# Router logits as column-group partial sums, and a first round whose table is read without the counts, in one step of a two-layer streaming encoder

## Chip, cores and metric

The kernel runs on one core of a Trainium2 chip, in one launch that takes the whole inference step. The metric is device time in microseconds (us) of that core; lower is better. All data are float32, so each matmul of the program stands in the trace as two records.

## What is computed

One step of an encoder with DEPTH = 2 layers, for 512 prompt tokens and 32 sample tokens (544 rows of 1024). A layer is a combined input projection, three parallel mixers (differential attention, retention, convolution), an output projection with a layer norm, a mixture of experts, a second layer norm and a gated side input. The part that the change touches is the router and what follows from it:

```python
def moe(x, w_router, b_router, w_exp_gate, w_exp_up, w_exp_down):
    logits = (x @ w_router) + b_router            # (544, 16), w_router (1024, 16)
    scores = softmax(logits).reshape(N, 4, 4)
    # best group of four experts by the sum of its two best scores,
    # then the two best experts inside it, weights w = their scores / their sum
    for e in range(16):
        h = silu(x @ w_exp_gate[e]) * (x @ w_exp_up[e])
        y = y + gates[:, e:e + 1] * (h @ w_exp_down[e])
```

## The kernel before, in words

The rows are held as five tiles of the token axis: four of 128 rows and one of 32 (tile 4, the sample). Everything is ordered by hand: each engine runs its own list, and semaphores join them. The engines are PE (TensorE), ACT (ScalarE), DVE (VectorE), POOL (GpSimd) and SP (SyncE, which issues nearly all weight loads, 1 MB each).

**From the output projection to the router.** For each tile, in the order 0, 1, 4, 2, 3 (`MIX_ORDER`), PE computes the output projection in two halves (`product(t, n)`, L1131), DVE adds the residual and normalises the row tile (L1894, L1611 to L1621), PE transposes it (`turn_tile`, L852) and ACT copies the transpose into `xT` (`x1_turned`, L1363). Then `logits(t)` (L1116) multiplies: eight matmuls with the tile's transposed activations as the stationary operand (128 columns, 32 for tile 4) and the 16 columns of the router's weights `w_rt` as the moving one. Between them PE does `turn_prow` (L1172) and `project(t)` (L1181), products for the gated side input. PE's list has `product(2,0)`, `logits(0)`, `product(2,1)`, `logits(1)`, `product(3,0)`, `logits(4)`, `product(3,1)`, then the transposes of tile 2, `turn_prow`, `logits(2)`, `project(0)`, the transposes of tile 3, `logits(3)`, `project(1)`, `project(2)`.

**From the logits to the table.** DVE picks the experts (from L1936), PE counts and ranks the picked rows (`rank`, L1212 to L1214, behind `project(2)` on PE's list), DVE makes seat numbers and a table `ctl` (from L1957), and signals `routed` (L2032). A round of the expert stage treats two half tiles of 64 rows, a front one (slots of `ring`) and a back one (`back` in `region`); experts are walked from 0 upwards at the front and from 15 downwards at the back. `ctl` holds the number of rounds done so far (word 0), the number of rounds of this layer less one (word 1), and per round the front expert, the back expert and two flags that say whether each is new. `mid` is word 1, `base` word 0. There are 25 rounds in the two layers together.

**SP around the first round.** Before `routed`, SP has loaded experts 0 and 15 (`early`, L649 and L651), but for the back half of the down weights. After `routed` it loads `base` and `mid` into registers (L678, L679), waits for the four gate transfers (`hold` on `b_full`, `z_full`), and then `part_of("gate", 0)` reads four table words (L681) and issues four conditional loads (L693, L694), each behind a `hold` on the signal that the buffer has been read; a load whose flag is zero moves nothing but still signals. The same follows for "up". Then come the back down loads (L651), the wait for all down transfers, three loads of norm parameters (L708 to L710) and the loop over the other rounds. PE's first `gate(0)` (L1262, L1263) waits for the signals of the conditional gate loads, and each later product for those of its own round.

```python
hold(routed, l + 1)
base = e.value_load(ctl[0:1, 0:1], min_val=0, max_val=MAXROUND * (DEPTH - 1))
mid = e.value_load(ctl[0:1, 1:2], min_val=MINROUND - 1, max_val=MAXROUND - 1)
```

## Time and profile before

| What | Value |
| --- | --- |
| median of 3 runs | 1571.17 us (1570.41 to 1574.28) |
| profiled execution, its own time | 1564.81 us |
| its span | 1563.0 us |
| granted TensorE clock, mean over the span | 0.97 |
| PE matmul busy | 1431.6 us (92%), 6900 records |
| DVE busy | 574.2 us (37%) |
| ACT busy | 271.2 us (17%) |
| POOL busy | 118.0 us (8%) |
| DMA | 326.24 MB, mean 209 GB/s |

The span is the time between the first and the last instruction of the profiled execution; some 1.8 us lie around it. "Busy" counts the engine's own instructions, whether or not anything waits for them. The three timed runs are some 6 us longer than the execution that was profiled. Layer 0's stage from output projection to table ends at about 396.6 us of the span, layer 1's at about 1167.7 us; the expert stages follow them.

### The profile page before, as it was taken

What the parts mean: (1) busy time and instruction counts of PE and PEld (TensorE: products, weight loads), DVE (VectorE), ACT (ScalarE), POOL (GpSimd) and SP (SyncE); (2) the same over time, 40 slices, a digit from 0 to 9 for tenths busy, and PEclk for the clock granted to TensorE, in tenths of its full rate; (3) what the DMA queues carried; (4) which work ended last, traced back from release to release, by engine and by line L of the source; (5) the groups of instructions that cost most, each with busy time, mean ns of one, the idle gap of its engine ahead of it and who ended that gap; (6) DMA issues with size and microseconds to landing.
All of it is one profiled execution on the core that took longest, in us unless ns stands there. A gap on an engine that the chain in (4) does not pass through costs nothing.

```text
span 1563.0 us, 20264 instructions
## 1 busy us (share of the span) xinstructions
PE 1431.6 (92%) x6900; PEld 753.4 (48%) x6900; DVE 574.2 (37%) x1144; ACT 271.2 (17%) x655; POOL 118.0 (8%) x133
## 2 busy tenths in 40 slices
PE   7999998999899999995999999979979999978688
PEld 3786356554344444332458854555543444323244
DVE  5085874254210111005522958553441111001156
ACT  1201243212100100010121023431121100000112
POOL 2100001010100000004000000010100000000120
PEclk9999998999999999997999999999999999999889
DMA  8623011343399989997033221023434899999731
GB/s 292 225 97 124 1 54 58 135 178 136 136 377 424 386 312 391 427 424 259 1 123 106 85 84 54 3 75 145 179 121 164 335 340 365 426 427 426 286 123 44
DMA packets 81802, 326.24 MB, mean 209 GB/s; under 512 B 12652, under 2 KB 15012, under 8 KB 56396
## 3 DMA queue, kind: packets, MB, share of 16 engines
q1 hardware_dynamic: 67492, 278.47, 46.2%
q0 software_dynamic: 9136, 29.16, 5.1%
q10 hardware_dynamic: 5112, 17.80, 2.8%
q8 instruction: 37, 0.61, 0.2%
q14 instruction: 25, 0.20, 0.0%
HBM read 429.19 MB, written 30.19 MB: 294 GB/s over the span
## 4 chain that ended last, share of the span: by engine, by line
PE 76%; DMA 9%; issue 5%; DVE 4%; SPq 3%; ACT 2%; DVEq 1%; POOL 0%; ACTq 0%
PE psum L1262 15%; PE psum L908 11%; PE psum L1289 8%; PE psum L967 7%; PE psum L1323 7%; PE psum L1131 7%; DMA region<-in_w_exp_up_dram 5%; PE psum L882 4%; DMA region<-in_w_exp_gate_dram 2%; PE psum L852 2%; DMA region<-in_w_exp_down_dram 2%; PE psum L1181 2%; PE psum L831 1%; PE psum L1263 1%; SPq L681 1%
## 5 line engine op out<-in xcount | busy, mean ns | idle before, releaser
L1262 PE MATMUL psum<-ring,xT 128*64 128x512 f32 x800 | 359.2, 601 | 21.8 <-DMA region<-in_w_exp_gate_dram 9.0
L1263 PE MATMUL psum<-region,xT 128*64 128x512 f32 x800 | 360.3, 602 | 0.0
L1262 PEld LDWEIGHTS psum<-ring,xT 128*64 128x64 f32 x800 | 107.8, 139 | 228.0 <-issue 228.0
L1289 PE MATMUL psum<-ring,region 128*64 128x512 f32 x400 | 179.8, 602 | 10.3 <-DMA region<-in_w_exp_down_dram 5.7
L1290 PE MATMUL psum<-region 128*64 128x512 f32 x400 | 180.0, 602 | 0.0
L908 PE MATMUL psum<-xT,ring 128*128 128x272 f32 x768 | 176.5, 393 | 0.0
L908 PEld LDWEIGHTS psum<-xT,ring 128*128 128x128 f32 x768 | 145.8, 190 | 30.1
L2058 DVE COPY region<-psum 128x512 f32<-128x512 f32 x25 | 17.3, 692 | 341.2 <-PE psum L1290 341.2
L967 PE MATMUL psum<-ring,xT 128*128 128x512 f32 (+1 forms) x288 | 132.5, 603 | 7.2 <-DVE region L1733 7.2
L1323 PE MATMUL psum<-ring,xT 128*128 128x512 f32 x256 | 115.8, 610 | 1.5 <-issue 1.5
L746 POOL TENSOR_TENSOR rr<-rq,half 128x1 f32<-128x1 f32 (+3 forms) x39 | 54.8, 1406 | 754.6 <-DVE rq L1601 278.6
L1289 PEld LDWEIGHTS psum<-ring,region 128*64 128x64 f32 x400 | 54.9, 139 | 116.4 <-issue 116.1
L1263 PEld LDWEIGHTS psum<-region,xT 128*64 128x64 f32 x800 | 107.7, 138 | 0.0
L1683 DVE SCALAR_TENSOR_TENSOR region<-region,hwT 128x574 f32<-128x574 f32 x120 | 92.6, 814 | 4.5
L2048 DVE TENSOR_TENSOR region<-region,psum 128x512 f32<-128x512 f32 x25 | 17.2, 688 | 192.0 <-PE psum L1263 192.0
L967 PEld LDWEIGHTS psum<-ring,xT 128*128 128x128 f32 (+1 forms) x288 | 49.2, 181 | 75.4 <-issue 62.7
L1323 PEld LDWEIGHTS psum<-ring,xT 128*128 128x128 f32 x256 | 49.4, 196 | 61.1 <-issue 58.8
L1363 ACT ACTIVATE xT<-psum 128x512 f32<-128x512 f32 (+1 forms) x60 | 29.5, 531 | 239.8 <-PE psum L852 239.3
L852 PE MATMUL psum<-ident,x 128*128 128x128 f32 (+1 forms) x240 | 31.9, 279 | 35.4 <-issue 34.7
L1363 ACT ACTIVATE region<-psum 128x512 f32<-128x512 f32 (+5 forms) x74 | 35.2, 519 | 156.5 <-PE psum L919 60.3
L1131 PE MATMUL psum<-ring,region 128*128 128x512 f32 x128 | 60.3, 615 | 1.4 <-ACT region L1492 0.7
L882 PE MATMUL psum<-ring,xT 128*128 128x512 f32 x128 | 59.9, 621 | 0.7 <-issue 0.7
(260 smaller groups left out, 1489.0 us busy)
## 6 DMA issues: line engine op xcount, KB each, us to landing
region<-in_w_exp_gate_dram SPq DMA_DIRECT2D x54, 1024.0 KB
ring<-in_w_exp_gate_dram SPq DMA_DIRECT2D x54, 1024.0 KB
region<-in_w_exp_up_dram SPq DMA_DIRECT2D x54, 1024.0 KB
ring<-in_w_exp_up_dram SPq DMA_DIRECT2D x54, 1024.0 KB
ring<-in_w_exp_down_dram SPq DMA_DIRECT2D x54, 1024.0 KB
region<-in_w_exp_down_dram SPq DMA_DIRECT2D x54, 1024.0 KB
ring<-in_w_in_dram SPq DMA_DIRECT2D x24, 1024.0 KB, 7.4
expert_results<-region ACTq DMA_DIRECT2D x25, 512.0 KB
```

The lines of the kernel that those rows point to most:

```text
L852: m = pe.transpose(B(key)[:, q * ROWS[t]:(q + 1) * ROWS[t]], x[0:ROWS[t], t, (4 * s + q) * P:(4 * s + q + 1) * P], ident[0:ROWS[t], 0:ROWS ...
L882: m = pe.matmul(B(key)[0:ROWS[t], :], xT[:, kc, span(t)], slot(u)[:, kc % 4, :], start=kc == 0, stop=kc == KC - 1)
L908: m = pe.matmul(B(key)[:, 0:HALF], w, xT[:, kc, half * HALF:(half + 1) * HALF], start=kc == 0, stop=kc == KC - 1)
L967: m = pe.matmul(bank[g - 1][0:ROWS[t], :], xT[:, 4 * half + kc, span(t)], slot(w)[:, kc, :], start=half == 0 and kc == 0, stop=half == 1 a ...
L1131: m = pe.matmul(B(key)[0:ROWS[t], :], mixT[kc][:, span(t)], slot(u)[:, kc % 4, :], start=kc == 0, stop=kc == KC - 1)
L1262: pe.matmul(bank[b][front, :], xeT[:, kc, front], ring[:, BLOCK_SLOT[u], kc % 4, :], start=kc == 0, stop=kc == KC - 1)
L1263: m = pe.matmul(bank[b][last, :], xeT[:, kc, last], back[:, UNIT_ROOM[u], kc % 4, :], start=kc == 0, stop=kc == KC - 1)
L1289: pe.matmul(bank[5 + half][front, :], hT[:, 2 * n + q, front], ring[:, BLOCK_SLOT[u], 2 * q + half, :], start=n + q == 0, stop=n + q == 2)
L1290: m = pe.matmul(bank[5 + half][last, :], hT[:, 2 * n + q, last], back[:, UNIT_ROOM[u], 2 * q + half, :], start=n + q == 0, stop=n + q == 2)
L1323: m = pe.matmul(B(key)[0:ROWS[t], :], xT[:, kc, span(t)], slot(u)[:, kc % 4, :], start=kc == 0, stop=kc == KC - 1)
L1363: sc.activation(dst, src, func).then_inc(free[use(key)], 1)
L1683: m = ve.scalar_tensor_tensor(cT[:, s, :], src, hwT[:, s, 32 + j:33 + j], cT[:, s, :], ALU.mult, ALU.add)
```

## The change

Router: `w_rt` is padded with zeros to 32 columns per chunk and becomes the stationary operand; `xT` becomes the moving one (128 columns, 32 for tile 4). The eight chunks go to four column groups of the array, two chunks accumulated in each, so that four partial sums stand in 4 x 32 partitions of one PSUM bank (`part_sums`). ACT copies them into SBUF (`parts_copied`), and one more matmul with the copy as stationary operand and a constant of four stacked identities, `gather4`, as moving one adds the four parts and turns them (`logits`). The new copy of tile t is issued on ACT behind `x1_turned(t)`, and PE has other work between `part_sums(t)` and `logits(t)`, except for tile 3.

SP: `base` is no longer read but carried in a register from the layer before (`rounds_done`); the holds on the gate transfers stand ahead of the wait for `routed`; the holds on read buffers are left out for round 0; `mid` is read just ahead of the loop. Around it: one more memset on POOL and one more small constant load on SP at the start, SP's wait for the memsets moved ahead of the constants' loads, and two small buffers and two counting semaphores put together.

```diff
+    c["gather4"] = (np.arange(P)[:, None] % 32 == np.arange(NE)[None, :]).astype(np.float32)
...
-        w_rt = sb("w_rt", [P, KC, NE])
+        w_rt = sb("w_rt", [P, KC, 32])
+        gather4 = sb("gather4", [P, NE])
...
+                base = rounds_done
+                for n in range(2):
+                    hold(b_full[BLOCK_SLOT[("gate", n)]], 16 * (base + l + 1))
+                    hold(z_full[BLOCK_SLOT[("gate", n)]], 16 * (base + l + 1))
                 hold(routed, l + 1)
-                base = e.value_load(ctl[0:1, 0:1], min_val=0, max_val=MAXROUND * (DEPTH - 1))
-                mid = e.value_load(ctl[0:1, 1:2], min_val=MINROUND - 1, max_val=MAXROUND - 1)
...
-                        hold(read, base + k + 1)
+                        if not first:
+                            hold(read, base + k + 1)
...
                 e.dma_start(bple, a["b_ple_gate"][L].to_broadcast([P, D])).then_inc(ln2p_in, 16)
+                mid = e.value_load(ctl[0:1, 1:2], min_val=MINROUND - 1, max_val=MAXROUND - 1)
+                rounds_done = base + mid + 1
...
+            pl.memset(w_rt[:], 0.0)
...
-                def logits(t):
+                def part_sums(t):
                     for s in range(2):
                         turned(l, ("x1", t, s))
-                    key = ("logit",)
-                    if t == MIX_ORDER[0]:
+                    key, r, n = ("logit",), ROWS[t], MIX_AT[t]
+                    if n == 0:
                         room(l, key)
+                    else:
+                        pe.wait_ge(lp_done, TILES * l + n)
                     pe.sem_inc(pe_pass, 1)
-                    for kc in range(KC):
-                        m = pe.matmul(B(key)[0:ROWS[t], NE * t:NE * t + NE], xT[:, kc, span(t)], w_rt[:, kc, :], start=kc == 0, stop=kc == KC - 1)
-                    if t == MIX_ORDER[-1]:
+                    for j in range(2):
+                        for g in range(4):
+                            m = pe.matmul(B(key)[32 * g:32 * g + 32, P:P + r], w_rt[:, 2 * g + j, :], xT[:, 2 * g + j, span(t)], start=j == 0, stop=j == 1)
+                    m.then_inc(lp_full, 1)
+
+                def logits(t):
+                    key, r, n = ("logit",), ROWS[t], MIX_AT[t]
+                    pe.wait_ge(lp_done, TILES * l + n + 1)
+                    pe.sem_inc(pe_pass, 1)
+                    m = pe.matmul(B(key)[0:r, NE * t:NE * t + NE], part_logits[:, n % 2, 0:r], gather4[:], start=True, stop=True)
+                    if n == TILES - 1:
                         m.then_inc(full[use(key)], 1)
...
+                def parts_copied(t):
+                    n = MIX_AT[t]
+                    sc.wait_ge(lp_full, TILES * l + n + 1)
+                    sc.activation(part_logits[:, n % 2, 0:ROWS[t]], bank[LOGIT_BANK][:, P:P + ROWS[t]], ACT.Copy).then_inc(lp_done, 1)
```

PE's list from `product(2,1)` of layer 0 on, before:

```order
L1116 MATMUL psum<-w_rt,xT 128x16 x8
L852 MATMUL psum<-ident,x 128x32 x8
L1131 MATMUL psum<-ring,region 128x512 x4
L1131 MATMUL psum<-ring,xT 128x512 x4
L1116 MATMUL psum<-w_rt,xT 32x16 x8
L1131 MATMUL psum<-ring,region 128x512 x4
L1131 MATMUL psum<-ring,xT 128x512 x4
L852 MATMUL psum<-ident,x 128x128 x8
L1172 MATMUL psum<-ident,region 128x128 x8
L1172 MATMUL psum<-ident,region 128x32 x2
L1116 MATMUL psum<-w_rt,xT 128x16 x8
L1181 MATMUL psum<-region 128x512 x4
```

The same stretch in the change, where L864, L1153, L1194 and L1203 are the lines that were L852, L1131, L1172 and L1181:

```order
L1138 MATMUL psum<-gather,region 128x16
L1131 MATMUL psum<-xT,w_rt 32x128 x8
L864 MATMUL psum<-ident,x 128x32 x8
L1153 MATMUL psum<-ring,region 128x512 x4
L1153 MATMUL psum<-ring,xT 128x512 x4
L1138 MATMUL psum<-gather,region 128x16
L1131 MATMUL psum<-xT,w_rt 32x32 x8
L1153 MATMUL psum<-ring,region 128x512 x4
L1153 MATMUL psum<-ring,xT 128x512 x4
L1138 MATMUL psum<-gather,region 32x16
L864 MATMUL psum<-ident,x 128x128 x8
L1194 MATMUL psum<-ident,region 128x128 x8
```

Each group of eight router matmuls keeps its place; the adding matmul of a tile stands one product later, that of tile 2 behind `project(0)`, and that of tile 3 directly behind its part sums.

SP's list from the last early load to the first conditional one, before:

```order
L649 DMA ring<-in_w_exp_down_dram 128x2048 x2
L678 TENSOR_LOAD ctl
L678 ISA x2
L679 TENSOR_LOAD ctl
L679 ISA x2
L508 ISA
L681 TENSOR_LOAD ctl
L681 ISA x2
```

and in the change, there and ahead of the loop:

```order
L654 DMA ring<-in_w_exp_down_dram 128x2048 x2
L688 TENSOR_LOAD ctl
L688 ISA x2
...
L719 DMA region<-in_b_ple_gate_dram 128x1024
L720 TENSOR_LOAD ctl
L720 ISA x2
L722 UNCONDITIONAL_BRANCH
```

One load of `ctl` and its register work are gone, and the other stands behind the parameter loads.

## Rows read from the trace of the kernel before

**Rows 1.** The page, part 4: shares of the chain that ended last.
```profile
PE 76%; DMA 9%; issue 5%; DVE 4%; SPq 3%; ACT 2%; DVEq 1%; POOL 0%; ACTq 0%
```

**Rows 2.** Timeline of PE, layer 0: start, length, engine, line, operation, count, idle before.
```profile
328.99 1.06 PE L831 MATMUL psum<-ring,region 128*32 128x128 f32 x32
329.87 1.06 PE L831 MATMUL psum<-ring,xT 128*32 128x128 f32 x32
330.85 1.09 PE L852 MATMUL psum<-ident,x 128*128 128x128 f32 x8
...
338.65 1.85 PE L1116 MATMUL psum<-w_rt,xT 128*128 128x16 f32 x16
340.35 1.07 PE L852 MATMUL psum<-ident,x 128*128 128x128 f32 x8
...
357.58 0.68 PE L1116 MATMUL psum<-w_rt,xT 128*32 128x16 f32 x16
358.19 3.70 PE L1131 MATMUL psum<-ring,region 128*128 128x512 f32 x8
...
367.24 1.96 PE L1116 MATMUL psum<-w_rt,xT 128*128 128x16 f32 x16
369.05 3.68 PE L1181 MATMUL psum<-region 128*128 128x512 f32 x8
372.56 1.04 PE L852 MATMUL psum<-ident,x 128*128 128x128 f32 x8
374.44 1.93 PE L1116 MATMUL psum<-w_rt,xT 128*128 128x16 f32 x16 [0.84 <-ACT xT L1363]
```

**Rows 3.** Timeline of DVE, layer 0, tile 3's norm, first router operation, first after the rank.
```profile
369.58 1.28 DVE L1621 SCALAR_TENSOR_TENSOR x<-x,rr,region 128x1024 f32<-128x1024 f32 x1 [0.44 <-POOL rr L746]
...
376.40 0.22 DVE L1936 TENSOR_TENSOR region<-psum,b_rt 128x64 f32<-128x64 f32 x1 [5.52 <-PE psum L1116]
...
385.24 0.17 DVE L1957 TENSOR_SCALAR ints<-psum 128x16 int32<-128x16 f32 x1 [3.50 <-PE psum L1214]
```

**Rows 4.** Timeline of ACT, layer 0: second copy of tile 3's transpose, first half of gathered rows.
```profile
373.73 0.60 ACT L1363 ACTIVATE xT<-psum 128x512 f32<-128x512 f32 x1
...
399.21 0.60 ACT L1537 ACTIVATE xT<-psum 128x512 f32<-128x512 f32 x1 [2.79 <-PE psum L1241]
```

**Rows 5.** Groups by line and form: an ACT pass of 128 columns out of PSUM.
```profile
L1340 ACT ACTIVATE region<-psum 128x128 f32<-128x128 f32 x32 | 8.4, 286 | 0.0
```

**Rows 6.** Chain that ended last, layer 0 behind the table: start, length, what.
```profile
396.64 0.47 SPq L678
...
397.46 0.28 SPq L679
...
398.03 0.05 SPq L508
...
398.41 0.26 SPq L681
...
406.85 7.39 DMA region<-in_w_exp_down_dram
...
434.11 12.62 DMA region<-in_w_exp_gate_dram
```

**Rows 7.** Timeline of PE, starts of expert products that waited for SP's loads.
```profile
401.49 1.09 PE L1262 MATMUL psum<-ring,xT 128*64 128x512 f32 x1 [1.88 <-DMA region<-in_w_exp_gate_dram]
...
446.97 0.61 PE L1262 MATMUL psum<-ring,xT 128*64 128x512 f32 x1 [0.88 <-DMA region<-in_w_exp_gate_dram]
...
1191.87 0.61 PE L1262 MATMUL psum<-ring,xT 128*64 128x512 f32 x1 [0.37 <-DMA region<-in_w_exp_gate_dram]
```

**Rows 8.** PE by stretches: length, busy, granted clock, DMA share, GB/s.
```profile
376.00:380.00 4.00, 4.00 (x9) 0.59 0.01 4
1120.00:1124.00 4.00, 4.00 (x6) 0.60 0.14 33
600.00:700.00 100.00, 93.86 (x440) 0.99 1.01 424
```

More of the change, by code:

```diff
@@ L703, in _ @@
                     for n in range(2):
-                        hold(b_full[BLOCK_SLOT[(name, n)]], 16 * (base + l + 1))
-                        hold(z_full[BLOCK_SLOT[(name, n)]], 16 * (base + l + 1))
+                        if name != "gate":
+                            hold(b_full[BLOCK_SLOT[(name, n)]], 16 * (base + l + 1))
+                            hold(z_full[BLOCK_SLOT[(name, n)]], 16 * (base + l + 1))
                     if name != "down":
-                        part_of(name, 0)
+                        part_of(name, 0, True)
                 e.dma_start(lnp_near[:, 0, :], a["ln2_g"][L].to_broadcast([P, D])).then_inc(ln2p_in, 16)
@@ L750, in _ @@
             pl.memset(ones[:], 1.0)
-            pl.memset(hw[:], 0.0).then_inc(hw_zero, 1)
-            pl.memset(zero, 0.0).then_inc(zeroed, 1)
+            pl.memset(w_rt[:], 0.0)
+            pl.memset(hw, 0.0).then_inc(hw_zero, 1)
+            pl.memset(zero, 0.0).then_inc(hw_zero, 1)
             pl.iota(iota[:], [[1, P]], base=0, channel_multiplier=0, allow_small_or_imprecise_dtypes=True)
@@ L1187, in _ @@
                 product(2, 0)
-                logits(0)
+                part_sums(0)
                 turn_tile(l, "x1", x1_ready, 1)
                 product(2, 1)
-                logits(1)
+                logits(0)
+                part_sums(1)
                 turn_tile(l, "x1", x1_ready, 4)
                 product(3, 0)
+                logits(1)
+                part_sums(4)
+                product(3, 1)
                 logits(4)
-                product(3, 1)
                 turn_tile(l, "x1", x1_ready, 2)
@@ L1199, in _ @@
                     turn_prow(t)
+                part_sums(2)
+                project(0)
                 logits(2)
-                project(0)
                 turn_tile(l, "x1", x1_ready, 3)
+                part_sums(3)
                 logits(3)
@@ L1515, in _ @@
                     sample_out("wo", n)
-                for t in MIX_ORDER[:-1]:
+                def parts_copied(t):
+                    n = MIX_AT[t]
+                    sc.wait_ge(lp_full, TILES * l + n + 1)
+                    sc.activation(part_logits[:, n % 2, 0:ROWS[t]], bank[LOGIT_BANK][:, P:P + ROWS[t]], ACT.Copy).then_inc(lp_done, 1)
+                for n, t in enumerate(MIX_ORDER[:-1]):
                     x1_turned(t)
+                    if n < 3:
+                        parts_copied(t)
                 for t in range(TILES):
@@ L1712, in _ @@
                 filled(l, key)
-                ve.tensor_copy(tails[:].rearrange("p a b -> p (a b)"), B(key)[0:CW - 1, :]).then_inc(free[use(key)], 1)
+                ve.tensor_copy(tails.rearrange("p a b -> p (a b)"), B(key)[0:CW - 1, :]).then_inc(free[use(key)], 1)
                 ve.drain()
```

25 lines of the change are left out of this document (15 added, 10 removed).

## The prediction

> **What bounds the kernel now.** I read the shares of the chain that ended last first, then the timelines around the router, then SP's part of the chain. The chain is three quarters PE; SP's own instructions hold 3% of it and DMA 9% [rows 1]. So PE's time counts wherever PE has no gap, and SP's where PE waits for a load signal.
>
> In the stage ahead of the table PE runs without a gap from product to product; the first idle time is 0.84 us ahead of the last router group, where it waits for ACT's copy of tile 3 [rows 2]. DVE has tile 3's norm done at 369.58 + 1.28 = 370.86, but PE transposes that tile only at 372.56 [rows 2, 3]: PE is 1.7 us late, so what PE saves ahead of that point arrives in full. Behind the logits PE is late again: DVE waited 3.50 us for the rank, which stands behind two projections on PE's list [rows 3]. From there DVE alone leads to the table, and then SP to PE: `gate(0)` starts at 401.49, 1.88 us after PE had nothing to do, because SP's signals come at that time [rows 7].
>
> **Router, per tile.** A 128-row group takes its slot from 338.65 to 340.35, 1.70 us for 16 records, 0.106 us each [rows 2]. For tile 1, which is followed by transposes of 32 rows, I add 0.10 for the change of shape (below): 1.80. Tile 4's group holds 357.58 to 358.19, 0.61, plus 0.10 on each side: 0.81. Tile 2's holds 367.24 to 369.05, 1.81 [rows 2].
>
> The new groups are not in the trace, but their like is: the sample's projections use 32 stationary columns in four column groups with 128 moving ones. 32 such records go from 328.99 to 329.87, 0.88 us, and the last 32 up to the next shape take 330.85 - 329.87 = 0.98 [rows 2]. So 16 records are 0.44, and a change of shape costs 0.10. One comes at each end: 0.64 per part sum. The same matmuls in sequence at the old group's 0.106 per record would take 1.70, the other bound of a group. Tile 4's part sums (32 moving columns) I take at 0.44 too, since 16 records of 16 columns behind 32 stationary ones held 0.61 with their edges. The adding matmul has the old group's shape: two records, 0.21; that of tile 4 with 32 stationary columns, two records and two edges, 0.27.
>
> *Here a rule speaks against the change.* The Trainium skill, "TensorEngine Tiling (Array Packing)", section Tiling Modes, says that a change of tiling mode drains TensorE. The trace agrees in kind, and its price is the 0.10 us above. The same page, under Performance Considerations, has a matmul of one column take as long as one of 60. An estimate from it, at 2.4 GHz, is 16 x 60 / 2400 = 0.4 us for the old group too, and the change would then gain nothing on PE. The slot of 1.70 us says otherwise, so the row decides.
>
> *Up to the end of `product(3,1)`*: before 1.70 + 1.80 + 0.81 = 4.31. After: 0.64, then 0.21 + 0.64, then 0.21 + 0.64 = 2.34. Saved 1.97. *Then up to tile 3's transposes*: before 1.81; after 0.27 + 0.64 + 0.21 = 1.12. Saved 0.69; PE is 1.7 - 0.7 = 1.0 us late there and so still decides. *Tile 3*: before, from the end of ACT's copy (373.73 + 0.60 = 374.33) to DVE's first operation (376.40) 2.07 us [rows 3, 4]. After: start of PE 0.11 later (as 374.44 stands to 374.33), 0.44 with the length of the last record 0.18 (1.06 - 0.88), signal 0.07, ACT's copy 0.286 [rows 5], start 0.11, two records 1.93 - 14 x 0.106 = 0.45, signal 0.03: 1.68. Saved 0.4. ACT has nothing queued ahead of that copy but tile 3's own, and its four other new copies lie under a product or projection of PE. The 3.50 us that DVE waits for the rank is cover: PE's projections behind tile 3 start earlier by the same 0.4. **Sum 3.1 us a layer**; the end bounds are 1.5 (the shape changes three times as dear) and 4 (no edges at all).
>
> **SP, per layer.** From 396.64 to 398.41 lie two table loads and four holds, 1.77 us [rows 6]. The first load behind the wait costs 0.47 where a later one costs 0.26; that surcharge of 0.21 goes to whichever load is first, so 1.56 are saved. The holds are (398.41 - 398.08) / 4, some 0.08 each, and four more go from the first gate and up parts: 0.3. Back comes `mid`, 398.03 - 397.46 = 0.57, behind the parameter loads. So `gate(0)`'s signals come 1.56 + 0.08 = 1.64 earlier, at 399.85; the first half of the gathered rows is turned and copied at 399.21 + 0.60 = 399.81 [rows 4], and that ties: nothing beyond 1.6 could be had. The down loads are issued 1.86 earlier and last 7.39 as before [rows 6]; SP waits for them, then does its parameter loads, `mid` and the loop. From there SP is 1.86 - 0.57 = 1.3 ahead.
>
> That smaller number decides. In layer 1 SP's signal sets `gate(1)` at 1191.87, with 0.37 us of idle PE before it; in layer 0 SP's run of instructions goes on to the gate load of round 2, issued at 434.11, which lands 12.62 later and lets PE start at 446.97 after 0.88 us of idling [rows 6, 7]. PE's own 1.6 is more than 1.3 in both. **1.3 us a layer**, between 0 (the start of the stage is hidden by something I don't see) and 1.6.
>
> **Whether it lasts.** Later in a layer the loads fill the DMA engines, 1.01 of them over 600 to 700 us, at 424 GB/s [rows 8]. Each of these loads is released by PE's reading of the buffer before it, and the stretch starts from PE's own pace, so I let the whole chain shift. If a fixed rate from a fixed start held, SP's start of that stream moves by the same 1.3.
>
> **Costed at nothing.** The extra memset and the constant's small load at the start: PE first reads either at 338.65 [rows 2], and SP's weight loads behind them, pushed back by one issue, are covered by the input projections before; if that cover is gone, an issue or two, under 2 us once, is the price. The shared buffers and semaphores change no order.
>
> **Sum.** 2 x (3.1 + 1.3) = 8.8 us. The profiled execution took 1564.81, so 1556.0 by that; the three runs have their median 6.4 us above it, so **1562.4** against 1571.17.
>
> **Rivals.**
> - *The clock gives back more.* PE has a granted clock of 0.59 over 376 to 380 and 0.60 over 1120 to 1124, that is 1.2 GHz for most of it, each time behind a router group [rows 2, 8]. With (1 - 0.59) x 4 = 1.6 us lost in each, 1.6 to 3.3 more is saved if the shorter groups end one or both: 1559 to 1561. For it: they stand behind just the work that shrinks. Against: the idle time ahead of tile 3's group stays, and a new one of some 0.5 us joins it behind the part sums, which could as well bring such a stretch.
> - *Only half arrives.* If another wait sits behind PE in the router stage (DVE's 1.0 us margin, a bank that ACT frees late) or the expert stage swallows the 1.3, 3 to 5 us is left: 1566.5 to 1568. That is no difference from before.
> - *The part sums don't overlap.* If with 32 stationary columns each of the 16 records took its full 0.27 (the length at the end of such a group, 1.06 - 0.88 + 0.1), a tile would cost 4.4 + 0.4 instead of 1.7: 3 us more on each of five tiles and two layers, 30, less 2.5 from SP: 1599, slower. It decides from 0.09 us per record upwards. Against it: 32 such records in 0.88 us, in the same four groups.
> - *The change doesn't do what it says*, that is SP loads both words as before: then 6.2 is left, 1565. The listed order speaks against it.
>
> **How the numbers follow.** Forecast as summed 0.62, clock on top 0.14, half or less 0.19, no overlap or another loss 0.05. A difference of 0.3%, 4.7 us, is about what a measurement of this kernel can tell from none, so "faster" means below 1566.5: 0.62 + 0.14 = 0.76; same 0.19; slower 0.05. The range goes down by the clock's 3.3 and by the upper bounds of the terms, 2 x (0.9 + 0.3), to 1556, and one more for the spread of the runs, 1555; up it goes past the half gain to 1569.
>
> **What would show it.** Part sums of a 128-row tile in 0.4 to 0.5 us; PE's transposes of tile 3 some 1.0 us behind DVE's norm of it, where it was 1.7; 1.7 us between ACT's last copy of tile 3 and DVE's first router operation; `routed` 3.1 us earlier in layer 0 and 3.1 + 1.3 + 3.1 = 7.5 earlier in layer 1; SP's first gate signal 3.3 us behind `routed` instead of 4.8; `gate(1)` of layer 1 still waiting for SP. I am wrong if PE's busy groups shrink and `routed` doesn't move, or if the expert stage of a layer gets longer by what its start gained.

## The result, and the profile after

The changed kernel takes 1562.76 us, the median of six runs (1557.57 to 1564.57); the kernel before took 1571.35 beside it (1570.41 to 1576.75, six runs). The medians differ by 8.6 us. The ratio of the means is 0.9934 with a 95% interval of 0.9914 to 0.9955, that is 10.4 us less, with 7 to 14 allowed. The forecast was 1562.4.

The total came as forecast, its two halves did not: the router's part gave more than was summed, SyncE's part nothing that could be measured. That the two errors cancel is luck.

The two profiled executions can't be compared by their spans, 1563.0 and 1562.7 us: that of before was faster than all six of its timed runs. So I compare stages, each from its own start. By the page of the profile PE is busy for 1428.0 us (1431.6 before), ACT for 274.1 (271.2), and the mean clock is 0.967 (0.970). First the shares of the chain that ended last, after the change, from the page's part 4; they are those of before [rows 1] within one point.

```profile
PE 76%; DMA 10%; issue 5%; DVE 4%; SPq 2%; ACT 2%; DVEq 1%; POOL 0%; ACTq 0%
```

**The router stage.** The timeline of PE in layer 0 of the changed kernel, against [rows 2] (columns as there):

```profile
333.97 1.09 PE L864 MATMUL psum<-ident,x 128*128 128x128 f32 x8
...
341.86 0.65 PE L1131 MATMUL psum<-xT,w_rt 128*32 128x128 f32 x16
342.44 1.09 PE L864 MATMUL psum<-ident,x 128*128 128x128 f32 x8
...
350.24 0.29 PE L1138 MATMUL psum<-gather,region 128*128 128x16 f32 x2
350.46 0.64 PE L1131 MATMUL psum<-xT,w_rt 128*32 128x128 f32 x16
351.03 0.68 PE L864 MATMUL psum<-ident,x 32*128 32x32 f32 x8
...
372.57 0.29 PE L1138 MATMUL psum<-gather,region 128*128 128x16 f32 x2
372.71 1.07 PE L864 MATMUL psum<-ident,x 128*128 128x128 f32 x8
374.57 0.64 PE L1131 MATMUL psum<-xT,w_rt 128*32 128x128 f32 x16 [0.79 <-ACT xT L1390]
375.69 0.37 PE L1138 MATMUL psum<-gather,region 128*128 128x16 f32 x2 [0.48 <-ACT region L1546]
```

A part sum takes a slot of 342.44 - 341.86 = 0.58 us where the old group took 1.70. The adding matmul takes 0.22 ahead of a part sum and 0.14 ahead of transposes (0.17 for tile 4). From the first transposes of tile 0 to those of tile 3 it is now 38.74 us; before, 372.56 - 330.85 = 41.71. That is 2.97 less. DVE and ACT at tile 3, against [rows 3, 4]:

```profile
370.48 1.29 DVE L1657 SCALAR_TENSOR_TENSOR x<-x,rr,region 128x1024 f32<-128x1024 f32 x1 [0.44 <-POOL rr L757]
...
376.09 0.23 DVE L1972 TENSOR_TENSOR region<-psum,b_rt 128x64 f32<-128x64 f32 x1 [4.30 <-PE psum L1138]
...
383.23 0.17 DVE L1993 TENSOR_SCALAR ints<-psum 128x16 int32<-128x16 f32 x1 [1.81 <-PE psum L1241]
```

```profile
373.88 0.59 ACT L1390 ACTIVATE xT<-psum 128x512 f32<-128x512 f32 x1
375.27 0.28 ACT L1546 ACTIVATE region<-psum 128x128 f32<-128x128 f32 x1 [0.80 <-PE psum L1131]
```

PE turns tile 3 at 372.71, 0.94 us behind DVE's norm (371.77) where it was 1.7. From ACT's last copy of tile 3 (374.47) to DVE's first router operation it is 1.62 us, where it was 2.07. And DVE waits 1.81 us for the rank where it waited 3.50: the projections ahead of it on PE ran at full speed this time. The windows show why, against [rows 8]:

```profile
376.00:380.00 4.00, 4.00 (x11) 1.85 (x11) 3.22 (x12) 1.25 (x3) 0.00 (x0) 1.00 0.06 19
1120.00:1124.00 4.00, 4.00 (x10) 1.71 (x9) 3.38 (x5) 0.06 (x1) 1.52 (x1) 1.00 0.14 33
390.00:394.00 4.00, 4.00 (x11) 0.96 (x12) 3.23 (x16) 0.24 (x1) 1.09 (x1) 0.57 0.10 13
1185.00:1192.00 7.00, 5.26 (x14) 1.76 (x16) 1.24 (x3) 0.00 (x0) 0.56 (x1) 0.53 0.46 169
```

A slow stretch is a few microseconds in which the granted clock is near 0.5, that is 1.2 GHz. The two of before, at 0.59 and 0.60 over their windows, are gone. Others have come: one on PE's last projection ahead of the expert stage (390 to 394, clock 0.57; layer 1 has one at the same place, 5.25 us long), one behind an idle time of PE at the second round of layer 1 (1185 to 1192, clock 0.53). The first and the last stand in the next view, PE's timeline around the first round of layer 0 and at the second round of layer 1, against [rows 7]:

```profile
390.16 5.27 PE L1203 MATMUL psum<-region 128*32 128x512 f32 x8
398.04 1.14 PE L1268 MATMUL psum<-ident,xT 128*128 128x128 f32 x8 [2.60 <-issue]
399.73 0.61 PE L1289 MATMUL psum<-ring,xT 128*64 128x512 f32 x1 [0.55 <-ACT xT L1573]
```

```profile
1186.73 1.09 PE L1289 MATMUL psum<-ring,xT 128*64 128x512 f32 x1 [3.62 <-DMA region<-in_w_exp_gate_dram]
```

`gate(0)` no longer waits for SP, but comes late by PE itself: the projection took 5.27 us, and in both profiles of the kernel before 3.62. At `gate(1)` of layer 1 PE now waits 3.62 us for SP where it waited 0.37. The chain of waits of layer 0 shows SP's way there, against [rows 6]:

```profile
394.63 0.47 SPq L688
...
397.39 0.11 SPq L701
...
402.71 0.34 SPq L656
403.10 8.54 DMA region<-in_w_exp_down_dram
411.73 0.33 SPq L717
...
413.06 0.27 SPq L720
```

### The profile page after: what moved, and what is told of

Read it like the earlier page. It is cut to its first block, busy times and chain, and to the rows that moved or that the text cites. A ratio compares the mean times of both kernels' runs of the same rounds, so it can differ in the third digit from the quotient of the medians.

```text
span 1562.7 us, 20317 instructions
## 1 busy us (share of the span) xinstructions
PE 1428.0 (91%) x6920; PEld 743.8 (48%) x6920; DVE 574.4 (37%) x1144; ACT 274.1 (18%) x665; POOL 118.5 (8%) x134
## 4 chain that ended last, share of the span: by engine, by line
PE 76%; DMA 10%; issue 5%; DVE 4%; SPq 2%; ACT 2%; DVEq 1%; POOL 0%; ACTq 0%
PE psum L1289 15%; PE psum L920 11%; PE psum L1316 8%; PE psum L979 8%; PE psum L1350 7%; PE psum L1153 7%; DMA region<-in_w_exp_up_dram 6%; PE psum L894 4%; DMA region<-in_w_exp_down_dram 2%; PE psum L864 2%; PE psum L843 1%; PE psum L1203 1%; PE psum L1290 1%; DMA region<-in_w_exp_gate_dram 1%; PE psum L964 1%
## 5 line engine op out<-in xcount | busy, mean ns | idle before, releaser
L979 PE MATMUL psum<-ring,xT 128*128 128x512 f32 (+1 forms) x288 | 137.6, 622 | 7.2 <-DVE region L1769 7.2
L864 PE MATMUL psum<-ident,x 128*128 128x128 f32 (+1 forms) x240 | 32.1, 280 | 35.4 <-issue 34.6
L1153 PE MATMUL psum<-ring,region 128*128 128x512 f32 x128 | 58.6, 600 | 1.4 <-ACT region L1519 0.7
```

The source lines that it names most:

```text
L864: m = pe.transpose(B(key)[:, q * ROWS[t]:(q + 1) * ROWS[t]], x[0:ROWS[t], t, (4 * s + q) * P:(4 * s + q + 1) * P], ident[0:ROWS[t], 0:ROWS ...
L979: m = pe.matmul(bank[g - 1][0:ROWS[t], :], xT[:, 4 * half + kc, span(t)], slot(w)[:, kc, :], start=half == 0 and kc == 0, stop=half == 1 a ...
L1153: m = pe.matmul(B(key)[0:ROWS[t], :], mixT[kc][:, span(t)], slot(u)[:, kc % 4, :], start=kc == 0, stop=kc == KC - 1)
```

## Where SP's lead goes

I take `routed` as the start of DVE's last write of `ctl`, here in layer 0 before and after:

```profile
396.42 0.13 DVE L2032 CAST ctl<-cumf 1x1 int32<-1x1 f32 x1
...
394.41 0.13 DVE L2068 CAST ctl<-cumf 1x1 int32<-1x1 f32 x1
```

The next table, from the timelines of SP and DVE, has layers 0 / 1 in us behind `routed`: SP's first conditional gate load, the first of its back down loads, their landing (SP's next parameter load, where one stands there), and its first load of `gate(1)`. The rows below the third are experiments, told further down.

| Kernel, layer | gate(0) loads | down issued | down landed | gate(1) loads |
| --- | --- | --- | --- | --- |
| before, 0 / 1 | 4.53 / 4.97 | 10.03 / 10.62 | 17.90 / 19.23 | 22.76 / 23.72 |
| after, 0 / 1 | 2.98 / 2.95 | 8.30 / 8.82 | 17.32 / 18.60 | 22.67 / 23.66 |
| after, second profile | 2.97 / 2.96 | 8.30 / 8.98 | 17.73 / 18.02 | 23.07 / 23.07 |
| router_only | 4.53 / 4.97 | 10.03 / 10.61 | 17.76 / 18.39 | 22.63 / 22.88 |
| sp_only | 2.99 / 2.95 | 8.30 / 8.81 | 19.76 / 17.19 | 25.12 / 22.22 |
| parts_twice | 2.98 / 2.95 | 8.30 / 8.82 | 18.05 / 16.44 | 23.40 / 21.48 |
| mid_in_wait | 2.98 / 2.96 | 8.29 / 8.83 | 17.40 / 18.11 | 22.18 / 22.58 |
| params_in_wait | 2.98 / 2.95 | 8.30 / 8.82 | - | 20.67 / 21.06 |
| down_sooner | 2.98 / 2.95 | 4.35 / 4.81 | 13.21 / 13.28 | 18.58 / 18.44 |
| gate_first | 2.97 / 2.96 | 8.30 / 8.42 | - | 14.22 / 15.07 |

In layer 0 of the change SP starts 1.55 us sooner (4.53 - 2.98) and issues the down loads 1.73 sooner. Their landing takes 8.54 instead of 7.39 us, 1.15 back. `mid` and its follow-up take another 0.5 back. 1.73 - 1.15 - 0.5 is 0.1, and the row says 22.76 - 22.67 = 0.09. Layer 1 has 1.80 - 1.2 - 0.55 and ends at 0.06. The whole lead is gone when `gate(1)` is to be loaded. The second profile of the change has the `gate(1)` loads at 23.07 in both layers.

The lead is not lost everywhere. In layer 1 of sp_only and of parts_twice the `gate(1)` loads stand at 22.22 and 21.48, which is 1.50 and 2.24 sooner than before. Of the layers in which SP has its new order and its old way to `gate(1)`, these are the two in which PE's last projection took 3.62 us; in the others it took 5.25 to 6.45. Behind a quick projection PE turns the first rows early, POOL issues its gather of the next rows 3.4 us ahead of the down loads, and these land after 8.38 and 7.62 us. In layer 0 of the change the gather was issued 1.05 us ahead of them (in layer 0 of before 4.36):

```profile
402.09 1.00 POOL L785 DMA_INDIRECT xT<-mixed_rows,seat  x1 [2.03 <-issue]
...
401.66 1.00 POOL L797 DMA_INDIRECT xT<-mixed_rows,seat  x1 [2.03 <-issue]
```

So the slow last projection and the lost lead go together in these layers. What that is worth in time is for the experiments.

## Experiments

Theory A was the forecast: both parts arrive, the router's with 6.2 us and SP's with 2.6. Theory B: the router's part arrives, SP's is given back on the way to `gate(1)`.

**router_only** and **sp_only** split the change. The first takes back SP's order (its main lines; the holds of round 0 on read buffers and the place of `mid` go back as well):

```diff
-                base = rounds_done
-                for n in range(2):
-                    hold(b_full[BLOCK_SLOT[("gate", n)]], 16 * (base + l + 1))
-                    hold(z_full[BLOCK_SLOT[("gate", n)]], 16 * (base + l + 1))
                 hold(routed, l + 1)
+                base = e.value_load(ctl[0:1, 0:1], min_val=0, max_val=MAXROUND * (DEPTH - 1))
+                mid = e.value_load(ctl[0:1, 1:2], min_val=MINROUND - 1, max_val=MAXROUND - 1)
```

> The change without its part on SyncE: SP reads both words and holds all buffers behind `routed`, as before. Theory A (both gains arrive, as forecast: router 6.2 us in two layers, SP 2.6): 2.6 us slower than the changed kernel, 1565 us where before takes 1571.3. Theory B (SP's lead is given back inside the expert stage, because the back down loads, issued earlier, land later beside POOL's gather and because `mid` is read ahead of gate(1)): within 1 us of the changed kernel, 1562 to 1563.5. In the trace, both: `routed` some 3 us earlier than before behind the layer's attention stage, and gate(0) 1.9 us later behind `routed` than in the changed kernel. B alone: turn_rows(1) no later than in the changed kernel although gate(0) is.

Measured: 1559.77 us (ten runs), ratio to before 0.9938 (0.9917 to 0.9958). The whole change has 0.9934 and, in a second measurement, 0.9942. By the ratio the router's part alone is worth 9.7 us (6.6 to 13), and SP's part on top of it nothing, though the intervals would still allow the 2.6 of theory A. The time is under the 1562 to 1563.5 of theory B too. `gate(0)` starts 5.06 and 5.53 us behind `routed`, as before (5.07 and 5.54). B's sign, `turn_rows(1)` no later than in the change, did not come clearly: it stands at 20.61 and 20.86 us behind `routed`, in the two profiles of the change at 19.20 / 18.91 and 21.36 / 21.15. Up to the third round the two kernels are level (table below).

> The kernel before with the part on SyncE alone. Theory A: 2.6 us faster than before, 1568.7. Theory B: within 1 us of before; the down loads of the back slots take a microsecond longer than 7.8 and 8.5 us from issue to landing, or gate(1) is reached with more idle time of PE ahead of it, 2 to 4 us in all, where before had 0.4 in layer 1. The time from `routed` to turn_rows(1) is then the same as before to 0.5 us, where A has it 1.3 shorter.

Measured: 1569.27 us (twelve runs), ratio 0.9991 (0.9975 to 1.0007). That is 1.4 us less, nearer to B, with the 2.6 us of A still inside the interval. The trace shows both halves of the story. In layer 1 the start comes as forecast: `gate(0)` 3.75 us behind `routed` instead of 5.54. At `gate(1)` PE stands for 1.76 us where it was 0.37. That takes 1.4 us of the lead back, and up to the third round 1.5 us of it arrive (65.98 for 67.48), about what A expected:

```profile
1176.39 0.74 PE L1269 MATMUL psum<-ring,xT 128*64 128x512 f32 x1 [0.54 <-DMA region<-in_w_exp_gate_dram]
...
1195.41 0.61 PE L1269 MATMUL psum<-ring,xT 128*64 128x512 f32 x1 [1.76 <-DMA region<-in_w_exp_gate_dram]
```

In layer 0 not even the start comes: a slow stretch lies on the last projection (6.39 us for 3.62), `gate(0)` starts 6.77 us behind `routed`, later than before, the down loads take 11.5 us, and the third round comes 2.5 us later (70.34 for 67.87). So neither theory is whole: in sp_only the lead arrives in the layer with the quick last projection, and is lost in the one with the slow.

```profile
392.89 6.39 PE L1188 MATMUL psum<-region 128*32 128x512 f32 x8
401.78 1.97 PE L1248 MATMUL psum<-ident,xT 128*128 128x128 f32 x8 [2.50 <-issue]
```

**before_again** and **after_again** are the two kernels unchanged, for second profiles.

> The kernel before, unchanged, for a second profile: which clock stretches stand at the same place in both profiles. If the stretches at 376 to 380 and 1120 to 1124 belong to the kernel they come again; if they are chance, the stage from the first turning of a layer to `routed` is up to 2 us shorter here. Time 1570 to 1575.

> The changed kernel, unchanged, for a second profile and a second interval. Both theories: 8 to 9 us faster than before, ratio 0.993 to 0.996. From the first turning of a layer to `routed` 60.4 and 60.5 us as in its first profile if no slow stretch falls there; gate(0) 5 us behind `routed`; PE idle for 2 to 4 us behind the first round, waiting for SP's gate(1) signal, in both layers, if theory B has the right wait.

Measured: 1572.11 us in one run, and 1560.24 (five runs), ratio 0.9942 (0.9918 to 0.9966). The stretches of the kernel before came again at their places, and the stage repeats to 0.02 us. This table is from the first transposes of tile 0 over DVE's first router operation to `routed`, layers 0 / 1, in us:

| Kernel | tile 0 to router | router to routed |
| --- | --- | --- |
| before | 45.55 / 47.25 | 20.01 / 20.11 |
| before, second profile | 45.55 / 47.25 | 20.01 / 20.09 |
| sp_only | 47.25 / 45.56 | 20.01 / 20.09 |
| after, both profiles, and router_only | 42.12 / 42.12 | 18.32 / 18.40 |
| parts_twice | 43.99 / 43.99 | 18.31 / 18.40 |

The numbers come in steps of 1.7: 45.55 and 47.25, 20.01 and 18.32. Each step is one slow stretch: the one at 376 to 380 us of before costs (1 - 0.59) x 4 = 1.6 us by its row in [rows 8], the level being 1.2 GHz for most of it. So the kernel before has three of them in the two layers' stages, in both profiles; the changed kernel has none. (gate_first_old_router, below, has 45.90 and 19.65 in layer 0: one stretch that lies across the boundary, with the same sum.) Without them the stage is 45.55 - 42.12 = 3.43 us shorter: that is the router's own work. For after_again I had expected 2 to 4 us of idle time at `gate(1)`; there are 0.57 and 0.79. There the slow stretch on the last projection took the whole of it (6.39 and 6.45 us), so PE came late enough for SP:

```profile
385.97 6.39 PE L1203 MATMUL psum<-region 128*32 128x512 f32 x8
394.90 1.96 PE L1268 MATMUL psum<-ident,xT 128*128 128x128 f32 x8 [2.54 <-issue]
```

The 9 us between the two spans of the changed kernel (1562.7 and 1553.4) are of this kind: 4.2 arise ahead of layer 0's router, 3.6 between the two layers' stages and 3.4 at layer 1's `gate(1)`, and later stretches take some back. The two executions ran the same instructions.

**parts_twice** measures the disputed matmuls:

```diff
-                    for j in range(2):
+                    for j in (0, 1, 0, 1):
```

> The changed kernel with each tile's part-sum matmuls done twice (the second time from the start again, the result is the same). If four column groups run side by side, 16 more records are 0.44 to 0.48 us for a tile of 128 rows and 0.25 for tile 4, all of it ahead of `routed`: 4 x 0.46 + 0.25 = 2.1 us a layer from the first turning to `routed`, 60.4 to 62.5, and 4.2 us in the total, 1564.4. If they don't run side by side, 0.11 each or more: 1.7 us a tile, 7 a layer. If something else than PE sets the stage, less than 1 a layer.

Measured: 1561.31 us (four runs), ratio 0.9931 (0.9912 to 0.995). The stage up to `routed` gets 1.87 us longer in both layers (62.30 for 60.44), close to the 2.1 expected:

```profile
341.29 1.08 PE L1131 MATMUL psum<-xT,w_rt 128*32 128x128 f32 x32
342.30 1.09 PE L864 MATMUL psum<-ident,x 128*128 128x128 f32 x8
```

32 records take a slot of 1.01, 16 take 0.58: 16 more are 0.44 us, 0.027 each. The four groups do run side by side, and what is left of the single slot, 0.14, is both changes of shape together. But the expected 4.2 us don't stand in the total: its median is 1.1 over after_again's and its ratio even lower, with intervals that allow 3 to 4 us more. A part of them is lost in the clock, for in layer 1 the last projection is quick in this profile, where both profiles of the change have a slow one:

```profile
1162.12 3.62 PE L1203 MATMUL psum<-region 128*32 128x512 f32 x8
```

So this run settles the price on PE, not the share that arrives.

**mid_in_wait**, **params_in_wait**, **gate_first** take things off SP's way behind the down loads, one after the other:

```diff
                         for n in range(2):
                             early("down", n, 1)
+                        mid = e.value_load(ctl[0:1, 1:2], min_val=MINROUND - 1, max_val=MAXROUND - 1)
+                        rounds_done = base + mid + 1
+                        e.dma_start(lnp_near[:, 0, :], a["ln2_g"][L].to_broadcast([P, D])).then_inc(ln2p_in, 16)
+                        e.dma_start(lnp_near[:, 1, :], a["ln2_b"][L].to_broadcast([P, D])).then_inc(ln2p_in, 16)
+                        e.dma_start(bple, a["b_ple_gate"][L].to_broadcast([P, D])).then_inc(ln2p_in, 16)
+                        part_of("gate", 1)
```

mid_in_wait has the first two of the new lines, params_in_wait the first five, gate_first all six; what they move is taken away below. In gate_first the loop becomes `part_of("down", k)`, `part_of("up", k + 1)`, `part_of("gate", k + 2)` over `mid - 1` rounds, with the last down, up, down behind it.

> The changed kernel with `mid` read right behind the issue of the back down loads, while SP waits for their landing. Theory B (the chain behind the back down loads sets gate(1)): the 0.57 us of the load leave that chain, SP's gate(1) signals come 0.5 to 0.6 us earlier behind the landing, and PE's idle time ahead of gate(1), 0.57 and 0.79 us in the second profile of the change, is nearly gone. In the total 0.6 to 1.2 us less than the changed kernel if layer 1 passes it on, under 0.6 if the loads of its last rounds swallow layer 1's half: 1559 to 1560 beside 1560.2. Theory A (SP's lead arrives whatever stands there) expects the same 1.1.

> As before, and the three norm parameter loads go there too, ahead of the wait for the down transfers. Theory B: another 1.3 to 1.5 us off the chain behind the landing, so gate(1) waits for nothing in either layer and PE's idle time there is 0; a slow stretch of the clock behind that idle time goes with it where there was one. Against it: the parameter loads (1.5 MB written in all) now share the DMA engines with the back down loads, so that those land up to 1.5 us later. Total 0.6 to 2 us under the changed kernel: 1558.2 to 1559.6. If the landing takes the gain back: 1560.

> In addition, the loads of gate(1) are issued ahead of the wait for the down transfers, and the loop takes down(k), up(k+1), gate(k+2). Theory B: PE finds gate(1)'s signals long there; beyond the last kernel nothing more is to be had in that place (idle time is 0 already), but in layer 0 the gate load of round 2, whose landing let PE wait 0.88 us before, keeps its place behind up(1) in the list, so the same wait may stay: 1558 to 1560. The rotated order issues each gate load behind up's of the round before; if a wait for a buffer of `up` then holds a gate load back, the later rounds get longer: above 1562, slower than the change.

Measured:

| Kernel | us (runs) | ratio to before | routed to third round, layers 0 / 1 |
| --- | --- | --- | --- |
| before (first profile) | - | - | 67.87 / 67.48 |
| sp_only | 1569.27 (12) | 0.9991 (0.9975 to 1.0007) | 70.34 / 65.98 |
| router_only | 1559.77 (10) | 0.9938 (0.9917 to 0.9958) | 67.69 / 66.65 |
| after, first profile | 1562.76 (6) | 0.9934 (0.9914 to 0.9955) | 67.97 / 70.19 |
| after, second profile | 1560.24 (5) | 0.9942 (0.9918 to 0.9966) | 67.95 / 66.83 |
| mid_in_wait | 1558.69 (4) | 0.9905 (0.9881 to 0.993) | 67.61 / 67.93 |
| params_in_wait | 1553.0 (5) | 0.9891 (0.9873 to 0.9908) | 65.50 / 66.27 |
| gate_first | 1553.62 (6) | 0.9877 (0.9856 to 0.9898) | 64.04 / 63.74 |
| gate_first_words_read (below) | 1551.39 (6) | 0.9881 (0.9861 to 0.9901) | 65.26 / 63.97 |

(The last column goes to the turning of the rows of round 3, `turn_rows(3)`. The kernels were measured beside different runs of the kernel before, so the ratios are what to compare.) The chain behind the down loads was what set `gate(1)`, and it was worth more than I had put down: by the ratios params_in_wait is 7 to 8 us under the change and gate_first 9 to 10, instead of 0.6 to 2. Up to the third round of the two layers params_in_wait saves 3.0 us against the second profile of the change and 6.4 against the first; where the rest arises was not followed. Two things are seen. In params_in_wait the back down loads land in 8.45 us although the parameter loads run beside them, so my "against" did not come. And with the idle time a slow stretch goes: PE reaches `gate(1)` of layer 0 with 0.34 us of idling and at full clock, where the changed kernel had 2.33 and slow matmuls behind it.

```profile
415.01 0.61 PE L1289 MATMUL psum<-ring,xT 128*64 128x512 f32 x1 [0.34 <-DMA region<-in_w_exp_gate_dram]
...
441.99 0.61 PE L1289 MATMUL psum<-ring,xT 128*64 128x512 f32 x1 [0.88 <-DMA region<-in_w_exp_gate_dram]
```

The same view of the changed kernel, layer 0:

```profile
417.62 1.09 PE L1289 MATMUL psum<-ring,xT 128*64 128x512 f32 x1 [2.33 <-DMA region<-in_w_exp_gate_dram]
```

With gate_first the wait of 0.88 us at 441.99, round 2's, goes as well: between 400 and 445 us PE's timeline has no idle time. What I feared of it, a gate load held up behind an up load in later rounds, doesn't show. mid_in_wait brings SP's `gate(1)` loads forward by 0.5 us in layer 0 and 1.1 in layer 1, half of the latter by an earlier landing, and is on its own no measurable step (its interval overlaps that of the change). PE's idle time ahead of `gate(1)`, which I had expected nearly gone, is 1.86 and 2.61 us in its profile.

**down_sooner** and **gate_first_down_sooner** move the back down loads ahead of the first round's up part:

```diff
-                for name in ("gate", "up", "down"):
-                    if name == "down":
-                        key = ("pp", 4, 1)
...
+                part_of("gate", 0, True)
+                key = ("pp", 4, 1)
+                hold(full[use(key)], taken(l, key) + 1)
+                hold(xe_full, 16 * (base + 1))
+                for n in range(2):
+                    early("down", n, 1)
...
+                part_of("up", 0, True)
```

> The changed kernel with one swap on SP: the back down loads are issued ahead of the first round's up part instead of behind it. Theory B1 (the landing got longer because POOL's gather of the next rows runs beside it): issued some 2 us sooner the loads land before most of the gather, 7.4 to 8 us after their issue instead of 8.5 to 9.3, and the whole chain behind them is 2 to 2.9 us earlier; PE's idle time ahead of gate(1) is 0 in both layers; 2 to 4 us less than the changed kernel, 1557 to 1559. Rival B2 (the landing is long whatever runs beside it, or the gather, pushed back, makes PE wait for its rows): chain 1.5 to 2 us earlier only, or a wait for `xe` ahead of turn_rows(1); 1558.5 to 1560.

> Both: gate(1)'s loads, `mid` and the parameter loads ahead of the wait for down, and the back down loads ahead of the up part. The idle time ahead of gate(1) was 0 with gate_first, so B expects no more from this: 1553 to 1554. If PE had another wait left there (down(0) for its back transfers), up to 2 us less.

Measured: down_sooner 1551.42 us (four runs), ratio 0.9876 (0.9851 to 0.9901); with gate_first 1550.53 (six runs), 0.9882 (0.9863 to 0.9902). One swap does what three moves did. Both are under what was expected (1557 to 1559, and 1553 to 1554). SP's queue in down_sooner, layer 0 (start, length, line, transfer):

```profile
397.80 0.07 SPq L702 DMA_DIRECT2D region<-in_w_exp_gate_dram  x1
398.07 0.82 SPq L656 DMA_DIRECT2D region<-in_w_exp_down_dram  x2
401.71 0.09 SPq L701 DMA_DIRECT2D ring<-in_w_exp_up_dram  x1
...
406.93 0.34 SPq L717 DMA_DIRECT2D xT<-in_ln_g_dram  x1
```

I had expected the loads 2 us sooner; they are issued 3.95 us sooner, since the up part with its four table words, four holds and four conditional loads is that long. Of the length of the landing I had expected a microsecond back. From the first issue to the landing it was 9.02 and 9.78 us in the change, and is 8.86 and 8.47: only part of it. The landing in all profiles goes with the distance to POOL's gather of the next rows. Where the gather was issued 3.2 us or more ahead of the down loads (before, router_only, layer 1 of parts_twice and of sp_only), the loads took 7.6 to 8.6 us in this count; where it was issued 2.2 ahead to 0.9 behind, 9.0 to 9.8, and 11.5 once; in down_sooner it was issued 2.6 and 3.6 behind. So B1's collision is in the rows, but no kernel took the gather itself away, and it stays argued. The Trainium skill, "DMA: Bandwidth & Descriptors", section Issuing engines are not separate DMA queues, says that transfers run on the same 16 DMA engines and interleave whichever engine issued them. The runs are in line with it: half a megabyte, the gather's size, at the 424 GB/s of [rows 8] is 1.2 us (an estimate), and from the first profile of before to that of the change the landing grew by 1.15 and 1.19 us. Between the second profiles it grew by 1.7 and 0.5.

**gate_first_words_read** and **gate_first_old_router** take one part of the change away at a time, on top of the relieved chain. The first has the diff of router_only; the second is the kernel before with SP's part of gate_first.

> The kernel gate_first, with both words read and all holds behind `routed` as before the change. Here the chain behind the back down loads has slack, so what SP's part of the change is worth at the start of the stage shows by itself. Theory A: gate(0) 1.6 us later behind `routed` in each layer, 3.2 us in the total, 1556.8. Theory B (PE itself is the later one where a slow stretch of the clock falls on its last projection, and an idle time ahead of gate(0) brings slow stretches of its own): 0 to 3.2 by where those stretches fall, gate(0) 5.1 to 5.5 us behind `routed` instead of 4.9 to 5.3: 1554 to 1556.

> The kernel before with SP's whole new order (early `base`, `mid`, parameter loads and gate(1) ahead of the wait for down), with the old router. If the router's part is worth what its stage lost, 3.43 us of work a layer and up to two slow stretches of 1.7, it is 7 to 12 us slower than gate_first: 1560.5 to 1565.5, and 6 to 11 faster than before. If the router's gain depends on the late SP chain: within 4 us of gate_first.

Measured: 1551.39 us (six runs), ratio 0.9881 (0.9861 to 0.9901), the same as gate_first within the intervals and under both expectations; and 1561.6 (six runs), 0.9943 (0.9924 to 0.9963), as expected. So SP's part of the change is worth nothing measurable in the faster kernel either (0.0004 of the time, 0.6 us), though up to the third round the profile of gate_first is 1.2 and 0.2 us ahead. The router is worth 0.0066 against gate_first, some 10 us, as in router_only. Why so little of SP's lead is left even here, where the chain behind it is relieved, the trace says for layer 0. PE's timeline of gate_first_words_read, then of gate_first:

```profile
385.58 3.62 PE L1200 MATMUL psum<-region 128*32 128x512 f32 x8
391.92 1.14 PE L1265 MATMUL psum<-ident,xT 128*128 128x128 f32 x8 [2.72 <-DMA xT<-mixed_rows,slots]
394.89 1.09 PE L1286 MATMUL psum<-ring,xT 128*64 128x512 f32 x1 [1.83 <-DMA region<-in_w_exp_gate_dram]
```

```profile
390.04 5.32 PE L1206 MATMUL psum<-region 128*32 128x512 f32 x8
397.86 1.14 PE L1271 MATMUL psum<-ident,xT 128*128 128x128 f32 x8 [2.50 <-issue]
399.55 0.61 PE L1292 MATMUL psum<-ring,xT 128*64 128x512 f32 x1 [0.55 <-ACT xT L1576]
```

With SP late, PE idles 1.83 us; with SP early, PE is late itself by a slow projection. `gate(0)` starts 5.06 us behind `routed` in the one and 5.26 in the other (layer 1: 5.16 and 4.93).

The five versions with a relieved chain and the new router (params_in_wait, gate_first, down_sooner, gate_first_down_sooner, gate_first_words_read) beat both kernels: 1550.5 to 1553.6 us, by the ratios some 7 to 10 us under the change. Their intervals overlap, so the runs don't rank them; down_sooner needs one swap only.

## Why the prediction came out right

**Its total and direction** held (1562.4; measured 1562.76, 0.9914 to 0.9955 of before), but by terms that erred in opposite directions, which is luck. In the two layers `routed` comes 5.1 + 6.8 = 12.0 us sooner after the start of its stage: 6.9 of work, where 6.2 was forecast, and 5.1 of slow stretches. The total shows 8.6 to 10.4 of it. From `routed` to the third round the first profile of the change gives 2.8 us back, the second none; what takes the rest was not found. Point by point:

- *Router per tile.* The slot of a part sum was put at 0.64 and is 0.58; the adding matmul at 0.21 and is 0.14 to 0.22. The price of a change of shape, 0.10, was too high: 0.14 for both edges of a part sum. Up to `product(3,1)`'s end 1.97 was forecast, and it is 2.13 (34.32 to 32.19 us from tile 0's transposes). From there to tile 3's transposes 0.69 was forecast and 0.84 measured. At tile 3, 0.4 was forecast, and 0.46 (3.84 to 3.38 from transposes to DVE) measured. The sum of 3.1 a layer is 3.43.
- *The cover behind the logits* was right in kind: DVE waited for the rank and PE's projections moved with the logits.
- *The clock* was a rival at 0.14, priced at 1.6 to 3.3 us. It is what happened up to `routed`: 1.7 us in layer 0, 3.4 in layer 1, 5.1 together. All ten profiles with the new router have no slow stretch in the stage; all four with the old one have three in the two layers. What the rival left out: a slow stretch came back on PE's last projection, 18 times in these 20 layers. And it puts both stretches behind a router group, which [rows 2, 8] show for layer 0 alone. In layer 1 of before the slow product starts at 1119.91, behind a router group and the transposes of tile 4.
- *SP's start* held: 1.55 to 2.0 us sooner against 1.64, the down loads 1.73 to 1.80 against 1.86, `mid` 0.5 against 0.57.
- *The failed step* is "The down loads are issued 1.86 earlier and last 7.39 as before". They lasted 8.54 in layer 0 and 9.31 in layer 1, where 7.39 and 8.12 stood before. The step ahead of it failed as well: that at the start PE and SP tie, so that the lead of `gate(0)` arrives. PE was behind by its own last projection, which the prediction took as unchanged: 5.27 and 5.25 us for 3.62. Where the projection was quick, in layer 1 of sp_only, 1.5 us arrived. Of the 2.6 us of SP's term the totals show 1.4 alone (0.9991), none beside the new router (0.9938 against 0.9934 and 0.9942), 0.6 in gate_first (0.9881 against 0.9877). Each of these intervals still allows the 2.6, so the totals don't exclude a microsecond or two; in both profiles of the change the stages show no lead left at `gate(1)` in layer 0.
- *What was costed at nothing* at the start of the program does not show: in all 14 profiles tile 0's transposes of layer 0 stand at 329 to 334 us, with the new router and the old alike.
- *The part sums in sequence*, 1599 at 0.05, fell: 0.027 us a record, with the bound at 0.09. *SP loads both words as before* fell too: the listed order and the 2.98 us show that it doesn't. *Only half arrives*, 0.19, was right in kind for SP (the expert stage took its lead) and wrong for the sum.
- *What would show it* named 3.1 and 7.5 us for `routed` in layers 0 and 1; from the stage's own start it is 5.1 and 6.8. The absolute 7.5 could not be read, because stretches of the clock in unchanged stages move it by more.

The rule of the Trainium skill that was weighed against the change, "TensorEngine Tiling (Array Packing)", Performance Considerations (one column costs as much as 60), spoke of the moving columns, and these weren't what took the time. The weight loads (PEld) of the old group in the kernel before, for a tile of 128 rows and for tile 4, and below them of the new one in the second profile of the change:

```profile
338.65 1.75 PEld L1116 LDWEIGHTS psum<-w_rt,xT 128*128 128x128 f32 x15 [0.24 <-issue]
...
357.58 0.58 PEld L1116 LDWEIGHTS psum<-w_rt,xT 128*32 128x32 f32 x16 [0.76 <-issue]
```

```profile
337.65 0.38 PEld L1131 LDWEIGHTS psum<-xT,w_rt 128*32 128x32 f32 x16 [0.76 <-issue]
```

15 loads of 128 stationary columns fill the whole slot of the old group, 0.117 us each. Tile 4's group moves the same 16 columns behind 32 stationary ones and takes a slot of 0.61 instead of 1.70 [rows 2]; so it was the width of the stationary operand that made the old group long. 16 loads of 32 columns take 0.38 in the new group.

The swap alone would not have been enough. 16 part-sum records are 0.44 us with four groups side by side, so each takes some 0.11 in its own group. One after the other they would be 16 x 0.11 = 1.76 us, an estimate from these rows, and nothing would be gained on a tile of 128 rows. No run has the swap without the column groups.

## What to carry to other kernels

- With narrow outputs let the narrow operand be the stationary one and spread the chunks over column groups. The first takes away the long weight load (0.117 us a record here), the second keeps the 128 moving columns from costing as much again.
- Ahead of an edit that makes an engine earlier, follow its list to the next wait that another engine feels, and ask what its transfers will then run beside. Here one swap of two blocks behind the edited place was worth as much as the whole change, and the edited place itself nothing measurable.
- Compare stages from their own start in two profiles of each kernel. In steps of 1.7 us the clock showed which part of a gain is work and which is a slow stretch that moved.

## Not expected of the hardware

- The stage from tile 0's transposes to `routed` repeats to 0.02 us between profiles of the same kernel, slow stretches included (65.57 and 65.56, 67.36 and 67.34), although the spans differ by 7 us.
- The last projection took 3.62 us in all four layers of the kernel before, and 4.8 to 6.5 in 18 of 20 with the new router. It looks as if a slow stretch that a stage loses came again behind it. But with the old router and SP's new order (sp_only, gate_first_old_router) it was slow in three of four layers too, and their router stages had lost no stretch. In all of them, and in the kernel before as well, 2.5 us in which PE waits for DVE stand ahead of it, so this idle time alone does not tell quick from slow. The cause is open.
- An idle time of 3.62 us at `gate(1)` was followed by a granted clock of 0.53 over 7 us, so it cost nearly twice what the wait shows.
